# The front of a convolution stage: two zero fills issued earlier, the residual row added by VectorE, separate replica buffers, and depthwise tiles split five to three

## What is computed

```
def conformer_conv(x, w1, b1, dw, dwb, g, bn, w2, b2):
    h = x @ w1 + b1                       # 1024 -> 2048
    a, gate = jnp.split(h, 2, axis=-1)
    h = a * jax.nn.sigmoid(gate)
    h = lax.conv_general_dilated(         # depthwise, 31 taps, causal
        h, dw[:, None, :], window_strides=(1,), padding=[(30, 0)], ...) + dwb
    h = jax.nn.silu(layer_norm(h, g, bn))
    return h @ w2 + b2

def deepnorm(x, sub, g, b):
    return layer_norm(ALPHA * x + sub, g, b)
```

## Time and profile before

| what | us |
|---|---|
| median of three runs | 1178.7 (1175.54 to 1180.32) |
| the profiled execution, whole | 1174.66 |
| its span, first to last instruction | 1173.0 |
| TensorE busy in the span | 952.7 |
| VectorE, ScalarE, GpSimd busy | 454.5, 169.4, 220.9 |
| mean granted clock of TensorE (1 is 2.4 GHz) | 0.901 |

### The profile page before, as it was taken

How to read it: one execution, slowest core, us unless ns; L and a number is a source line. 1 busy time by engine, 2 the same in 40 slices (tenths; PEclk the granted TensorE clock), 3 DMA queues, 4 the chain that set the end, 5 groups by cost and what they waited for, 6 DMA issues and landing times.

```text
span 1173.0 us, 13864 instructions
## 1 busy us (share of the span) xinstructions
PE 952.7 (81%) x5241; PEld 499.1 (43%) x5241; DVE 454.5 (39%) x925; ACT 169.4 (14%) x376; POOL 220.9 (19%) x314
## 2 busy tenths in 40 slices
PE   6999969983999698999379899878459977999930
PEld 3444324542555354554134454434235534555510
DVE  1799913553111011111586548564511101111126
ACT  0000021311000000001113332432020000000110
POOL 1094000024211111100431002021240212020022
PEclk8999989985999899999589999978679978999975
DMA  8994349964999999999640003201859999999932
GB/s 252 387 409 157 87 152 414 402 226 170 345 389 403 373 390 384 382 408 411 214 180 1 1 1 144 72 1 68 322 201 392 387 372 391 388 383 395 398 127 107
DMA packets 74301, 313.40 MB, mean 267 GB/s; under 512 B 8797, under 2 KB 19209, under 8 KB 57704
## 3 DMA queue, kind: packets, MB, share of 16 engines
q1 hardware_dynamic: 36752, 228.83, 51.1%
q10 hardware_dynamic: 27352, 55.35, 12.6%
q0 software_dynamic: 10112, 28.06, 6.9%
HBM read 252.48 MB, written 55.31 MB: 262 GB/s over the span
## 4 chain that ended last, share of the span: by engine, by line
PE 58%; DMA 18%; DVE 15%; issue 4%; ACT 2%; POOL 2%; SPq 1%; POOLq 0%; ACTq 0%; DVEq 0%
PE ps L605 20%; PE ps L615 10%; DMA wring<-in_moe_w_gate_dram 8%; DVE arena L859 7%; PE ps L711 7%; PE ps L550 5%; PE ps L730 5%; DMA wring<-in_moe_w_up_dram 3%; PE ps L508 3%; DMA arena<-in_moe_w_up_dram 2%; DMA wring<-in_conv_w_dram 1%; PE ps L756 1%; PE ps L768 1%; DMA xs_dram<-x_sb,place_i 1%; PE ps L782 1%
## 5 line engine op out<-in xcount | busy, mean ns | idle before, releaser
L605 PE MATMUL ps<-wring,arena 128*64 128x256 f32 x2016 | 246.6, 403 | 55.3 <-DVE arena L1011 28.2
L605 PEld LDWEIGHTS ps<-wring,arena 128*64 128x64 f32 x2016 | 152.0, 146 | 149.6 <-issue 56.4
L1536 POOL DMA_DIRECT2D arena<-xs_dram x172 | 91.4, 536 | 357.0 <-DVE arena L1011 336.1
L615 PE MATMUL ps<-wring,arena 128*64 128x512 f32 x560 | 126.7, 594 | 6.2 <-DVE arena L1046 5.7
L508 PE MATMUL ps<-arena,wring 128*128 128x512 f32 x256 | 113.0, 604 | 4.2 <-DMA wring<-in_conv_w_dram 4.2
L1032 DVE COPY arena<-ps 128x256 f32<-128x256 f32 x32 | 13.6, 424 | 251.3 <-PE ps L648 251.3
L859 DVE SCALAR_TENSOR_TENSOR arena<-arena,dwT 128x512 f32<-128x512 f32 x116 | 96.1, 901 | 0.0
L711 PE MATMUL ps<-wring,arena 128*128 128x512 f32 x192 | 86.3, 605 | 3.5 <-ACT arena L1384 2.7
L605 PE MATMUL ps<-arena 128*64 128x256 f32 x736 | 83.2, 380 | 0.8 <-DMA arena<-in_moe_w_up_dram 0.7
L508 PEld LDWEIGHTS ps<-arena,wring 128*128 128x128 f32 x256 | 49.5, 194 | 66.3 <-issue 66.3
L1522 POOL TENSOR_TENSOR rstd<-vareps,half 128x1 f32<-128x1 f32 x20 | 25.7, 1287 | 271.6 <-DVE vareps L875 265.9
(11 more groups left out here) (189 smaller groups left out, 884.6 us busy)
## 6 DMA issues: line engine op xcount, KB each, us to landing
wring<-in_moe_w_gate_dram SPq DMA_DIRECT2D x24, 2048.0 KB, 25.1
wring<-in_moe_w_up_dram SPq DMA_DIRECT2D x24, 2048.0 KB, 19.7
wring<-in_moe_w_down_dram SPq DMA_DIRECT2D x24, 2048.0 KB, 20.2
xs_dram<-zero ACTq DMA_DIRECT2D x2, 16384.0 KB, 65.1
arena<-in_moe_w_up_dram SPq DMA_DIRECT2D x8, 2048.0 KB, 27.9
arena<-in_moe_w_down_dram SPq DMA_DIRECT2D x8, 2048.0 KB, 20.3
arena<-in_moe_w_gate_dram SPq DMA_DIRECT2D x8, 2048.0 KB, 25.7
arena<-xs_dram POOLq DMA_DIRECT2D x172, 64.0 KB, 7.1
```

The lines of the kernel that those rows point to most:

```text
L605: mm = pe.matmul(ps[h * CAP:(h + 1) * CAP, bank, 0:256], act[:, k, :], w[:, k, h * 256:(h + 1) * 256], start=(k == 0), stop=(k == KD - 1))
L615: mm = pe.matmul(ps[h * CAP:(h + 1) * CAP, bank, :], act[:, j % 2, (j // 2) * CAP:(j // 2 + 1) * CAP], w[:, j, h * 512:(h + 1) * 512], sta ...
L1536: pool.dma_start(where[q * QROWS:(q + 1) * QROWS, :, :], xs_tiles[q, :, bass.ds(n, 1), :, :]).then_inc(signal, 16)
```

## The change

The diff does the following, in the order of the program:

- VectorE takes five depthwise tiles, TensorE three; the filter product on GpSimd and the pieces `dw_a` shrink accordingly, and the gate products get new places between the taps.
- SyncE waits for the last token tile of x before it issues the second slice of `conv_w1`.
- `dw_r` is loaded in two pieces, of the 640 columns that are needed.
- The twelve replica pieces have places of their own in slots 1 and 2; no replica waits for another tile. Tile 7's are issued half by SyncE and half by ScalarE.
- `conv_b2` is loaded right behind the small parameters. VectorE scales it by `1/ALPHA` and adds it to x while it would wait for group 0; GpSimd's eight operations go. The product is then added with `ALPHA * x + product` in one operation. The attention part is changed alike: GpSimd scales the row once and only adds.
- `clear_rows(1)` is issued by ScalarE behind the sigmoid of group 5, instead of behind the last depthwise copy.

```diff
-DVE_TILES = 4
+DVE_TILES = 5
...
+        DWG = SHIFTS * (KD - DVE_TILES)
+        wdw = wring[:, 0, 0:ROUNDS * DWG * GRP].rearrange("p (r g n) -> p r g n", r=ROUNDS, g=DWG)
+
+        FIT = KD * F // REPW
+
+        def shifted(c, q):
+
+            slot_of, at = divmod(SHIFTS * (c - DVE_TILES) + q, FIT)
+            return wring[:, 1 + slot_of, at * REPW:(at + 1) * REPW]
+
+        def replicate(eng, c, shifts):
+
+            eng.wait_ge(s_glu, c + 1)
+            for s in shifts:
+                for q in range(SHIFTS):
+                    eng.dma_start(shifted(c, q)[s * GRP:(s + 1) * GRP, :],
+                                  hpad[q * GRP:(q + 1) * GRP, c, s:s + REPW]).then_inc(s_rep[c - DVE_TILES], 16)
...
             conv_in(0, 1)
+            sp.wait_ge(s_x[T - 1], 16)
             conv_in(1, 1)
...
-            replicate(4)
-            replicate(5)
-            sp.wait_ge(s_g1, KD)
-            replicate(6)
-            sp.wait_ge(s_pec, 1)
-            replicate(7)
+            for c in range(DVE_TILES, KD):
+                replicate(sp, c, (0, 1) if c == KD - 1 else (0, 1, 2, 3))
...
+            dve.wait_ge(s_b2, 16)
+            own(dve.tensor_scalar(resrow, resrow, 1.0 / ALPHA, None, ALU.mult))
+            for t in range(T):
+                ins = dve.tensor_tensor(x_sb[:, t, :], x_sb[:, t, :], resrow, ALU.add)
+            own(ins)
+
             dve.wait_ge(s_prT, 1)
...
             taps(0, {18: 1})
-            taps(1, {4: 2, 22: 3})
-            taps(2, {7: 4, 26: 5})
-            taps(3, {10: 6, 28: 7})
+            taps(1, {8: 2, 28: 3})
+            taps(2, {15: 4})
+            taps(3, {5: 5, 26: 6})
+            taps(4, {14: 7})
...
-                    ins = dve.tensor_tensor(x_sb[:, t, h * 512:(h + 1) * 512], x_sb[:, t, h * 512:(h + 1) * 512],
-                                            ps[:, bank + h, :], ALU.add)
+                    half_x = x_sb[:, t, h * 512:(h + 1) * 512]
+                    ins = dve.scalar_tensor_tensor(out=half_x, in0=half_x, scalar=ALPHA, in1=ps[:, bank + h, :],
+                                                   op0=ALU.mult, op1=ALU.add)
...
-            act.dma_start(dw_r[:, :], conv_dw[0]).then_inc(s_small, 16)
+            taken_cols = slice(0, P * DVE_TILES)
+            act.dma_start(dw_r[0:16, taken_cols], conv_dw[0, 0:16, taken_cols]).then_inc(s_small, 16)
+            act.dma_start(dw_r[16:CW, taken_cols], conv_dw[0, 16:CW, taken_cols]).then_inc(s_small, 16)
...
+            act.dma_start(resrow, conv_b2[0].partition_broadcast(P)).then_inc(s_b2, 16)
...
                 if c == 0:
                     later_loads()
+                if c == 5:
+                    clear_rows(1)
+                if c == KD - 1:
+                    replicate(act, c, (2, 3))
...
-            clear_rows(1)
             act.wait_ge(s_rope, 2)
...
-            pool.wait_ge(s_x0T, T)
-            pool.wait_ge(s_rows, 16 * 8)
-            for t in range(T):
-                own(pool.tensor_scalar(x_sb[:, t, :], x_sb[:, t, :], ALPHA, None, ALU.mult))
-                pool.tensor_tensor(x_sb[:, t, :], x_sb[:, t, :], resrow, ALU.add).then_inc(s_xa, 1)
...
+            own(pool.tensor_scalar(resrow, resrow, 1.0 / ALPHA, None, ALU.mult))
+
             def residual(t):
                 full(pool, ("Xa", t))
                 full(pool, ("Xb", t))
-                own(pool.tensor_scalar(x_sb[:, t, :], x_sb[:, t, :], ALPHA, None, ALU.mult))
                 pool.tensor_tensor(x_sb[:, t, :], x_sb[:, t, :], resrow, ALU.add).then_inc(s_xb, 1)
```

More of the change, by code:

```diff
@@ L239, in trunk @@
         s_pecv = sem("s_pecv")
-        s_xa = sem("s_xa")
+        s_b2 = sem("s_b2")
         s_At = sem("s_At")
@@ L978, in table @@
                                   ALU.mult)
-            dve.wait_ge(s_rows, 16 * 8)
+            dve.wait_ge(s_rows, 16 * 7)
             n = 0
@@ L1141, in take @@
                     half_x = x_sb[:, t, h * 512:(h + 1) * 512]
-                    dve.tensor_tensor(half_x, half_x, ps[:, bank, :], ALU.add).then_inc(bank_read[bank - 5], 1)
+                    dve.scalar_tensor_tensor(out=half_x, in0=half_x, scalar=ALPHA, in1=ps[:, bank, :],
+                                             op0=ALU.mult, op1=ALU.add).then_inc(bank_read[bank - 5], 1)
                     if h == 1 and t == T - 1:
@@ L1235, in later_loads @@
                 act.wait_ge(s_w1[KD - 2], 32)
-                act.dma_start(resrow, conv_b2[0].partition_broadcast(P)).then_inc(s_rows, 16)
                 act.dma_start(rw[:, :, :], router_w.rearrange("(p k) e -> p k e", k=KD)).then_inc(s_rows, 16)
```

30 lines of the change are left out of this document (10 added, 20 removed).

## The result

The changed kernel takes 1191.78 us (median of 4 runs, 1189.33 to 1192.42); the kernel before, beside it on the same chip, 1177.12 (4 runs, 1174.18 to 1180.32). The ratio is 1.0106, 95% interval 1.0071 to 1.014: slower by about 1%. The forecast was 1175.5, range 1162.5 to 1183: wrong, and on the other side.

The account below looks back on a forecast made before the run. The front's chain up to the last depthwise copy was taken as the bound: 149.6 without the fill, plus 12.7 for it, makes 162.3, plus 0.4 behind; 3.2 us gained from the median of 1178.7 gives 1175.5, range 1162.5 to 1183.

Parts of the forecast that it names:

- Start: Convolution's first group: holding the second slice and splitting `dw_r` let TensorE start at 15.4, a gain of 2.8 us.
- The clock's 2.8 us: Group 0: with 1.4 us idle TensorE stays at 2.4 GHz, gaining 2.8 us more; low end none.
- Residual, five tiles: Front on VectorE: about 6 us of bias work costs nothing; taps end at 147.8, GpSimd's filter product costing 5.0.
- the mark: The last depthwise tile's copy, at 165.88 before; everything behind moves with it; forecast at 162.3.
- Three tiles on TensorE, without the fill: End of the front: 20.6 us from 126.5 if replicas are there; by their issue and landing TensorE ends at 149.6.
- The zero fill: Fill moved ahead of the depthwise replicas: delays them and gives back 12.7 us, from 149.6 to 162.3.
- The hold: SyncE's replica queue stands still while 4290 fill packets go, 21.5 us, to 126.2; then 40 transfers of 0.63.
- The fill's own times: Early fill: issued at 99.9, moving from 104.7, 41 us alone; with the replicas ending at 152.0 to 156.2.
- The order within a queue: ScalarE's half of tile 7's replicas stands behind the fill and lands at 153.3 to 157.5.
- the third: Rival, 0.12: SyncE's replica issues wait until the fill is through, or go one turn each; 1194 us.
- Neither: Rival, 0.25: replicas slip between the fill's packets; last depthwise copy at 149.6, or 152.4 with cold start; 1163 to 1166.
- Behind the mark: After the front: scale-and-add loses 0.3 to 0.4 us; attention stage taken as 0, ends -1.5 and +0.5.

Follow-up runs that it names:

- e6: e1 without SyncE's wait for the last tile of x ahead of the second weight slice; 1165.94 us.
- e7: e6 with the load of VectorE's taps (31 rows of 640 columns) in one transfer again; 1169.74 us.
- e15: The kernel before with only the taps' load of 31 rows split into two pieces, all 1024 columns kept; 1175.71 us.
- e1: The changed kernel with the second zero fill put back behind the last depthwise copy; 1164.28 us, ratio 0.9887 to the kernel before.
- e9: e1 with the four additions of the bias row, and the row's scaling, back on GpSimd; 1176.98 us.
- e5: The changed kernel with the second fill issued by ScalarE right behind its eight replica transfers of tile 7; 1163.49 us, ratio 0.9847.
- e11: e1 with the attention's half of the residual as in the kernel before; 1160.54 us, ratio 0.9823.
- e17: e6 with the attention's half of the residual as in the kernel before; 1164.71 us, ratio 0.9857.

## Why the prediction was wrong

*Start.* The first group started at 15.38 (15.4 forecast). The reason was half wrong: the hold of the second slice did nothing (e6), the split of `dw_r` did all (e7, e15). The clock's 2.8 us came in ten profiles of fourteen with an early start (group 0 took 14.00), not in the changed kernel's own (15.68), behind the same 1.38 us of idle time; so its groups end at 128.4, and e1's at 127.0, for the 126.5 forecast.

*Residual, five tiles.* Right: free on VectorE, taps' end 149.0 for 147.8, 4.6 us lost to the filter product for 5.0. That GpSimd's work on `x_sb` costs time at the mark is shown by e9, 10.8 us for four additions; the 18 that the prediction put on the kernel before, with eight operations, no run shows. The terms of its sum for five tiles and eight gate products make 109.8, not 109.7, and those for the clock 2.9, not 2.8, which changes nothing.

*Three tiles on TensorE, without the fill.* 149.6 forecast, 149.80 measured in e1.

*The zero fill: the step that failed.* "SyncE is held while 8192 - 3902 = 4290 packets go: 21.5 us, to 126.2", and 0.63 us each after that. Neither half was so. SyncE's second issue went out at 109.63 and its first replica had landed by 114.73, and each transfer went on costing 1.7 us until the fill was through. So 27 of SyncE's 40 transfers had been issued when the fill landed at 154.16, where I had all 40 out by 151.4. Tile 6's replicas were in at 159.87, not 147.8, TensorE took 16.67 us for the two tiles behind them, and the fill gave back 26.9 us, not 12.7.

The hold was read out of one weight transfer of the kernel before that moved nothing for 4.3 us. The changed kernel repeats this row: 4.6 us without a packet of SyncE's behind its first replica, and then packets, with three quarters of the fill still to come. So the 4.3 us were what a transfer waits at its start beside a fill, and I made of them a state of the queue that lasts until the fill's rest has been queued. Why a start takes that long and a landing 7.4 us, when the transfers pass at 1.7, is open.

*The fill's own times.* It was issued at 100.95 (99.9 forecast) and landed at 154.16 (152 to 156.2), the latter partly by luck: its first packet moved at 102.2, not 104.7, and its 8192 packets took 51 us beside some 27 slow replica transfers of SyncE's, not 41 and up to 10.5 more for 38. The order within a queue was right. ScalarE's first replica, issued at 137.06, landed at 152.67, and none of them moved a packet before 151.1; the last landed at 159.01 (153.3 to 157.5 forecast), ahead of tile 6's from SyncE, so it set nothing.

*The rivals.* What happened is the third, "wait until fill 1 is through, or one turn each", with 0.12, in its second form. Its number, 1194 for 1191.78 measured, is luck: it had 15.1 us lost at the mark, where 10.9 were, and the two terms of its formula are off in opposite ways (the fill ended at 154.2, not 145.7, and the mark was 22.6 behind it, not 33.5, since 27 of SyncE's transfers were out by then). "Neither", with twice the chance, had spoken of packets slipping in between; they do, at a price that it put at nothing.

*Behind the mark.* From the mark to the first expert product the kernels take 116.3 to 119.4 us, 119.0 before and 117.5 after, so a loss of 0.4 can't be seen. Later fills (e1, e5) end at 218 to 224 with nobody on the chain waiting. In the attention stage nothing speaks against the forecast of 0; the profiled execution of the kernel before, on which the sum was made, had with 307.2 us the shortest such stretch of all. Of the 14.7 us between the medians, 9.3 to 10.9 are there by the end of the front; the rest lies in stages that scatter by as much, and stays open.

## What to carry to other kernels

Before moving a long transfer, list the short ones that will be in flight beside it and price each one by its pace under load, not by its pace alone: here 26 issues of SyncE paid some 1.1 us each, beside a fill that nobody was waiting for. Cutting one load of 31 rows into 16 and 15 moved TensorE's start by 1.8 and 2.9 us here, so a load of such a shape in front of the first weights is worth a try in two pieces. And an engine that only adds rows in SBUF can cost the engine beside it more than it saves. A version with the fill behind the last replicas or behind the last depthwise copy beats both kernels: five such versions are at 0.982 to 0.989 of the kernel before, not told apart by their intervals.

## What the runs showed of the hardware

- Beside a 16 MB fill of 2 KB rows, transfers of 32 rows from SBUF to SBUF are issued every 1.5 to 1.7 us in place of 0.63 and land 6.7 to 8.0 us after issue in place of 2.0; halving their bytes lowers that by a tenth, and putting the fill on GpSimd's queue does not lower it. The first of them moves its first packet 4.6 us after issue in place of 1.3.
- ScalarE's replica, issued behind a fill on the same queue, kept ScalarE issuing for 7.53 us in place of 0.63 (e1) and moved nothing until the fill's packets were nearly through (issued 137.06, landed 152.67).
- Loading 31 rows in one piece delayed a neighbouring 0.5 MB load by 3.3 us against two pieces of 16 and 15 (17.39 for 14.12, 18.04 for 14.78).
- VectorE's `scalar_tensor_tensor` takes 2.83 us for 0.74 (512 wide) and 3.29 for 1.28 (1024 wide) beside GpSimd's `tensor_tensor`; beside GpSimd's `tensor_scalar` the 1024-wide one took 1.98.
- The same 863 matmuls of one stage took 224.5 or 234.1 us in two executions (e11, e17), at granted clocks of 0.85 and 0.82.
